# Laying out a two-layer decoder step with DMA transfers that share their engines, blocks of 3, 4, 4, 3, 3 tiles, and later norms all turned by DMA

## The chip, the cores and the metric

The kernel runs on all 8 cores of one Trainium2 chip. Each core takes one of 8 prompt sequences (2048 tokens) and 16 of 128 sample sequences (8 tokens each); the cores don't talk to each other. The metric is the device time of the slowest core in microseconds (us).

## The reference, cut to what matters

Two layers. Each has a mixer with three branches and a feed-forward part:

```python
hn = rms_norm(h, norm_mix)
proj = hn @ w_in                      # q, k, v, g_out, g_lr (rank 16), xp, u, vv, gates
g_log = log_sigmoid(g_lr @ w_gk2 + b_gk) / 16
o, s_new = gla_mix(q, k, v, g_log, s_gla, chunk)          # A: recurrence with a decaying state
branch_a = (rms_norm(o, gla_norm) * silu(g_out)) @ w_br_a
branch_b = pool_mix(xp, hist, ...) @ w_br_b               # B: trailing means 2/4/8/16, per-group map
branch_c = spatial_gate(gelu(u), gelu(vv), ...) @ w_br_c  # C: 128x128 map per chunk
h = h + (sig(ga)*branch_a + sig(gb)*branch_b + sig(gc)*branch_c) @ w_out
h = h + relu(rms_norm(h, norm_ffn) @ w_ff1)**2 @ w_ff2
```

A final RMSNorm gives y. D is 1024, the feed-forward width 4096. The states of the recurrence and of the pooling are outputs as well.

## The kernel before, in words

A core has 17 tiles of 128 tokens: tile 0 is the sample group, tiles 1 to 16 the prompt. Tiles are grouped into five blocks (`BLK`, L24), 3, 3, 3, 4 and 4 tiles; a projection that gives features on the partitions runs once per block, with 384 or 512 columns in the moving operand, so blocks set shapes and order, while the sum of the columns doesn't depend on them. All matmuls are bf16 and go through `pe_group` (its matmul is L454), all PE transposes through `pe_transposes` (L467), ACT's work through `act` (L417), VectorE's through `tt` (L425), `stt` (L428) and `vcopy` (L437).

Weights are read from HBM as f32 and cast to bf16 by transfers that GpSimd issues (POOL queue, `wload`, L675) into a ring of seven slots of 1 MB source each. The first two, the two halves of v, go in four quarters of 512 KB (`plq.dma`, L379). All other loads and stores are issued by SyncE (SP queue, L379 too).

A layer runs in stages: per block `gla_project` (rank-16 gate `wglr` and `wgk2`, v, k, q), `gla_gate` (output gate) and `gla_scan` (recurrence over the block's prompt tiles); beside them `gla_sample`, 32 steps for the sample group, each of which loads a state tile `Sf` (256 KB), casts it on GpSimd (`Sinb`), uses it on the PE and stores it; then per block `mix_block`, then twice `gate_block` over all blocks, `out_block`, and four rounds of `ff1` and `ff2`. Where the kernel starts, 17 tiles `xt` are loaded, normed to `xn`, turned on the PE and copied to `hn`, the normed activations with features on the partitions that every projection reads. The norms after `out_block` (`hx`) are turned on the PE for blocks 0 and 1 and by a DMA transpose for blocks 2 to 4; the norms after the last `ff2` of layer 1 (`fx`) are all turned by DMA. `xt` has three buffers, `xn` and `hx` two, PSUM eight banks.

The order on each engine is not the order of the source. Every operation is recorded as a node with its dependences and a cost, and `lay_out` places the nodes one by one where they could start first by those costs; each engine then gets its instructions in that order and runs them in order, waiting on semaphores. A transfer's cost there is its bytes over a rate, plus a latency; `dma_at` keeps one time per queue at which it is free, and where the other queue is busy too, half of that overlap is added. So a change of a cost, or of the blocks, moves instructions everywhere.

## Time and profile before

| | us |
|---|---|
| runs, not profiled | 2384.38, 2383.14 and one of 2616.1; median 2384.38 |
| the profiled execution, its own time | 2381.28 |
| its span (slowest core, core 5) | 2380.2 |
| spans of the other cores | 2371.6 to 2379.2 |
| PE busy in the span | 2323.0 (98%) |
| DVE, ACT, POOL busy | 1273.8, 886.3, 245.9 |

The profiled execution took 1.1 us more than the span of its slowest core, and 3.1 us less than the median of the runs. PE is TensorE; "busy" counts a matmul from its start to its modelled end, so neighbours overlap and a sum of durations is more than the time they take together. "Idle before" is what an engine stood still before an instruction, and the name behind it is what released it. PEclk, or clock, is the share of full TensorE speed that was granted: 1.00 is 2.4 GHz, and 0.50 is 1.2 GHz.

### The profile page before, as it was taken

To read this page: it belongs to the slowest core of one execution; us is meant where nothing else is said; L and a number is where in the kernel's file an instruction comes from. 1 tells how busy PE (TensorE), PEld (TensorE's weight loads), DVE (VectorE), ACT (ScalarE), POOL (GpSimd) and SP (SyncE) were. 2 spreads that over 40 slices of the span, in tenths; PEclk is the share of its full clock that TensorE was granted. 3 is DMA by queue.
4 is the path that set the end of the run, shared out by engine and by line. 5 is a ranking of instruction groups with operands and counts; after the bars stand their busy time and mean duration, and the time that the engine had idled before them with its cause. 6 is when DMAs were issued, how large, how long until landed. Compare 5 with 4: busy or idle time off the path is not lost.

```text
span 2380.2 us, 40912 instructions; the slowest of 8 cores (2371.6 to 2380.2 us)
## 1 busy us (share of the span) xinstructions
PE 2323.0 (98%) x13392; PEld 1236.5 (52%) x13392; DVE 1273.8 (54%) x2231; ACT 886.3 (37%) x1810; POOL 245.9 (10%) x266
## 2 busy tenths in 40 slices
PE   6899999999999999999999999999999999999998
PEld 4576555546445454545455555564554454545453
DVE  3787776444465444434567776744434644434355
ACT  3877753222233121212456678322222421211133
POOL 2123222000000000000012233200000000000000
PEclk9999999999999999999999999999999999999999
DMA  9554936154186040406492467451815642222112
GB/s 162 143 165 122 186 125 142 71 97 111 70 159 103 1 72 1 76 1 116 127 164 74 149 137 157 100 135 63 142 72 107 126 65 36 36 37 36 18 59 93
DMA packets 219415, 229.41 MB, mean 96 GB/s; under 512 B 54315, under 2 KB 203307, under 8 KB 216106
## 3 DMA queue, kind: packets, MB, share of 16 engines
q0 software_dynamic: 83584, 78.45, 23.8%
q1 hardware_dynamic: 135626, 148.35, 20.9%
q8 instruction: 113, 1.85, 0.3%
q14 instruction: 92, 0.75, 0.1%
HBM read 240.41 MB, written 55.05 MB: 124 GB/s over the span
## 4 chain that ended last, share of the span: by engine, by line
PE 91%; DVE 3%; issue 2%; ACT 2%; DMA 2%; POOL 0%; DVEq 0%; ACTq 0%; SPq 0%; POOLq 0%
PE ps L454 90%; DMA wring<-w_in 1%; PE ps L467 1%; DVE U L428 0%; DMA Sf<-sgla 0%; DVE Sf L428 0%; ACT rsg L417 0%; DVE tmp L428 0%; ACT L417 0%; ACT tmp L417 0%; DVE sqg L425 0%; DVE lv L815 0%; ACT Sb L417 0%; DVE pt L425 0%; ACT xj L417 0%
## 5 line engine op out<-in xcount | busy, mean ns | idle before, releaser
L454 PE MATMUL ps<-hn,wring 128*128 128x384 bf16 (+1 forms) x6400 | 1245.4, 347 | 7.8 <-DVE sgt L425 1.7
L454 PEld LDWEIGHTS ps<-hn,wring 128*128 128x128 bf16 x6400 | 621.6, 98 | 545.4 <-issue 13.4
L454 PE MATMUL ps<-wring,a 128*128 128x512 bf16 x2176 | 476.0, 379 | 0.2 <-DVE a L425 0.2
L417 ACT ACTIVATE rl<-ps 128x384 f32<-128x384 f32 (+1 forms) x320 | 169.9, 532 | 637.9 <-PE ps L454 522.2
L425 DVE TENSOR_TENSOR h<-h,ps 128x512 f32<-128x512 f32 x340 | 233.1, 687 | 277.1 <-PE ps L454 276.1
L454 PEld LDWEIGHTS ps<-wring,a 128*128 128x128 bf16 x2176 | 212.8, 98 | 255.1 <-issue 0.7
L425 DVE TENSOR_TENSOR a<-rl 128x384 bf16<-128x384 f32 (+1 forms) x320 | 194.9, 612 | 276.0 <-ACT rl L417 268.0
L417 ACT ACTIVATE sg<-ps 128x384 f32<-128x384 f32 (+1 forms) x240 | 127.9, 533 | 450.3 <-PE ps L454 322.3
L454 PE MATMUL ps<-wring,hn 128*128 128x256 bf16 (+1 forms) x1088 | 193.7, 330 | 12.2 <-DMA wring<-w_in 10.8
L425 DVE TENSOR_TENSOR tmp<-sg,ps 128x384 f32<-128x384 f32 (+1 forms) x160 | 97.3, 608 | 154.4 <-ACT sg L417 79.1
L454 PEld LDWEIGHTS ps<-wring,hn 128*128 128x128 bf16 x1088 | 105.2, 99 | 79.3 <-issue 15.3
L454 PE MATMUL ps<-OBs,wring 128*128 128x384 bf16 (+1 forms) x640 | 143.8, 347 | 0.0
L675 POOL DMA_DIRECT2D wring<-w_ff x32 | 28.0, 875 | 1047.2 <-PE ps L454 1047.2
L425 DVE TENSOR_TENSOR acc<-sg,ps 128x384 f32<-128x384 f32 (+1 forms) x80 | 48.5, 607 | 162.7 <-PE ps L454 162.7
L454 PE MATMUL ps<-H4s,wring 128*128 128x384 bf16 (+1 forms) x640 | 130.7, 347 | 0.0
L454 PE MATMUL ps<-wring,mg 128*128 128x512 bf16 x544 | 119.7, 379 | 0.0
L425 POOL TENSOR_TENSOR go<-tmp,go 128x512 bf16<-128x512 f32 x64 | 77.8, 1221 | 244.4 <-DVE tmp L428 213.0
L417 ACT ACT_TABLE_LOAD x71 | 91.1, 1283 | 26.4 <-PE ps L454 24.2
L454 PEld LDWEIGHTS ps<-H4s,wring 128*128 128x128 bf16 x640 | 62.5, 98 | 55.7 <-issue 0.3
L454 PEld LDWEIGHTS ps<-OBs,wring 128*128 128x128 bf16 x640 | 62.6, 98 | 55.0
L454 PEld LDWEIGHTS ps<-wring,mg 128*128 128x128 bf16 x544 | 52.8, 98 | 61.3
L428 DVE SCALAR_TENSOR_TENSOR tmp<-ps,vec_t,rsg 128x256 f32<-128x256 f32 x136 | 61.7, 477 | 28.6 <-ACT rsg L417 27.5
(137 smaller groups left out, 1777.6 us busy)
## 6 DMA issues: line engine op xcount, KB each, us to landing
wring<-w_ff POOLq DMA_DIRECT2D x32, 1024.0 KB, 13.1
wring<-w_in POOLq DMA_DIRECT2D x28, 1024.0 KB, 16.1
Sf<-sgla SPq DMA_DIRECT2D x64, 256.0 KB, 3.7
gla_s<-Sf SPq DMA_DIRECT2D x64, 256.0 KB, 2.8
H4s<-H_d SPq DMA_DIRECT2D x12, 768.0 KB, 8.5
OBs<-OB_d SPq DMA_DIRECT2D x12, 768.0 KB, 5.0
h_d<-h SPq DMA_DIRECT2D x17, 512.0 KB, 2.7
h<-h_d SPq DMA_DIRECT2D x17, 512.0 KB, 9.9
```

The costliest lines, as they stand in the source:

```text
L417: op(ACT, lambda: nc.scalar.activation(out=now(out), in_=now(in_), func=func, **kw), reads, writes, occ, 125.0, SETS.get(func))
L425: op(E, lambda: E.e.tensor_tensor(out=now(out), in0=now(in0), in1=now(in1), op=alu), reads, writes, occ, 90.0)
L428: op(DVE, lambda: nc.vector.scalar_tensor_tensor(out=now(out), in0=now(in0), scalar=scalar, in1=now(in1), op0=op0, op1=op1), reads, writes ...
L454: inst = nc.tensor.matmul(now(m[0]), m[1], m[2], start=m[3], stop=m[4], **kw)
L467: inst = nc.tensor.transpose(now(o), i, ident_ap)
L675: nc.gpsimd.dma_start(out=view, in_=src).then_inc(slot_sem[k], 16)
```

## The change

Six edits.

1. Blocks are 3, 4, 4, 3 and 3 tiles; the places in SBUF of the merged activations `mg` follow (`mkb`).
2. `lay_out` no longer keeps a free time per queue. A transfer enters its queue (`coming`), the queues that have something to move share the rate (`moving`), and a transfer lands (`landing`) and frees its successors when its bytes are through, plus a latency. The rates, and the cost of a DMA transpose (once its bytes instead of three times, and 1250 ns on the issuing queue), are new.
3. The rank-16 weights are padded to 32 columns on the host, so that one row of a partition is contiguous and the memset goes; they and `wgk2` are issued behind all four quarters of v.
4. `bsp` and `rep`, loads of 256 and 16 KB at the start, wait for tile 5's norm instead of a ring slot; the ring loads up to the second output-gate weight are recorded, and the gate on later `xt` loads begins, one tile later.
5. In `gate_block` the four small products that fold the pooling map into `w_br_b` (`fuse`) are recorded between the first gates instead of ahead of them.
6. All norms after `out_block` are turned by DMA.

```diff
-BLK = [(0, 3), (3, 3), (6, 3), (9, 4), (13, 4)]
+BLK = [(0, 3), (3, 4), (7, 4), (11, 3), (14, 3)]
-    w_glr = din("w_glr", [DEPTH, 128, KT, 16])
+    w_glr = din("w_glr", [DEPTH, 128, KT, 32])
...
-        dma_at = [4000.0] * 5
+        clock = 4000.0
+        coming = []
+        moving = {3: collections.deque(), 4: collections.deque()}
+        landing = []
...
+            upto = best[1] if best is not None else 1e12
+            while clock < upto and (coming or moving[3] or moving[4]):
+                on = [q for q in (moving[3], moving[4]) if q]
+                to = min([upto] + [clock + q[0][1] * len(on) for q in on] + ([max(clock, coming[0][0])] if coming else []))
+                for q in on:
+                    q[0][1] -= (to - clock) / len(on)
+                    if q[0][1] < 1e-6:
+                        m = q.popleft()[0]
+                        landing.append((to + m.lat, m.idx))
+                        landing.sort()
+                clock = to
...
             if n.byts:
-                at0 = max(dma_at[e], s + occ)
-                other = dma_at[7 - e]
-                work = n.byts / (290.0 if e == 3 else 150.0 if dma_at[4] < 20000.0 else 245.0)
-                both = max(0.0, other - at0)
-                dma_at[e] = at0 + (both + work - both / 2 if work > both / 2 else work * 2)
-                fin = dma_at[e] + (3500.0 if e == 3 else 2500.0)
+                coming.append((s + occ, n.idx, e, n.byts / (300.0 if e == 3 else 265.0) + 100.0))
+                coming.sort()
...
-            if turn:
-                n *= 3
-            record(self.E, fn, reads, writes, 500.0 if self.E is SP else 900.0, 0.0, byts=n, after=after)
+            record(self.E, fn, reads, writes, 1250.0 if turn else 500.0 if self.E is SP else 900.0,
+                   2000.0, byts=n, after=after)
...
-    mkb = [24, 30, 36, 42, 50]
+    mkb = [24, 30, 38, 46, 52]
...
-        memset(wglr.t[:, :, :], 0.0, [wglr])
...
-        plq.dma(wglr.t[:, :, 0:16], w_glr[l], writes=[wglr])
+        plq.dma(wglr.t[:, :, :], w_glr[l], writes=[wglr])
...
-        spq.dma(bsp.t[:, :, :], b_sp[l:l + 1].broadcast_to([128, 4, 128]), writes=[bsp], after=[slots[6]])
+        spq.dma(bsp.t[:, :, :], b_sp[l:l + 1].broadcast_to([128, 4, 128]), writes=[bsp], after=[hnB[5]])
...
-        if b == 0:
-            for g in range(4):
-                ps = psum()
-                pe_group([(ps.t[:, :], wpm.t[:, g, :], bbc[1][:, g, :], True, True)], [wpm, bbc[0]], [ps])
-                act(bbc[1][:, g, :], ps.t[:, :], AF.Copy, [ps], [bbc[0]])
+        def fuse(g):
+            ps = psum()
+            pe_group([(ps.t[:, :], wpm.t[:, g, :], bbc[1][:, g, :], True, True)], [wpm, bbc[0]], [ps])
+            act(bbc[1][:, g, :], ps.t[:, :], AF.Copy, [ps], [bbc[0]])
...
+                if b == 0 and pi == 0 and m4 > 1:
+                    fuse(2 * m4 - 4)
+                    fuse(2 * m4 - 3)
...
-            norm_to_hn(t, hB[t].t[:, :], hH[t], hj, hx[t % 2], turn=b >= 2)
+            norm_to_hn(t, hB[t].t[:, :], hH[t], hj, hx[t % 2], turn=True)
...
-        if t == 6:
+        if t == 7:
             wget(0, "g1")
-        spq.dma(xt[t % 3].t[:, :], rows(x_p, x_s, t), writes=[xt[t % 3]], after=[slots[4]] if t > 5 else ())
+        spq.dma(xt[t % 3].t[:, :], rows(x_p, x_s, t), writes=[xt[t % 3]], after=[slots[4]] if t > 6 else ())
...
-            wget(0, "v0")
+            wget(0, "v1")
             gla_consts(0)
```

In the two programs, all engines get the same instructions in number and shape but for these: the PE has 96 transposes of `hx` fewer, VectorE 12 copies to `hn` and one memset fewer, SP 12 DMA transposes more, and the two `wglr` loads have another shape. Three places show how the order moves. In these rows `wring` is the ring of weights, a count behind x is of instructions, and L479, L492, L450, L462 and L700 are in the changed program what L454, L467, L425, L437 and L675 are before.

On the PE at the program's start, before, from behind the third transpose on (128x256 are products of v, eight for each quarter and tile, and `xn` is turned for one tile in eight):

```order
L454 MATMUL ps<-wring,hn 128x256 x16
L454 MATMUL ps<-hn,wglr 32x384 x8
L454 MATMUL ps<-wring,hn 128x256 x16
L454 MATMUL ps<-glr,wgk_bf 128x384 x3
L467 MATMUL ps<-ident_bf,xn_71 128x128 x8
L454 MATMUL ps<-glr,wgk_bf 128x384
L454 MATMUL ps<-wring,hn 128x256 x24
L467 MATMUL ps<-ident_bf,xn_70 128x128 x8
L454 MATMUL ps<-wring,hn 128x256 x32
L467 MATMUL ps<-ident_bf,xn_71 128x128 x8
L454 MATMUL ps<-wring,hn 128x256 x16
L454 MATMUL ps<-hn,wglr 32x384 x8
```

And now, from that transpose itself on:

```order
L492 MATMUL ps<-ident_bf,xn_70 128x128 x8
L479 MATMUL ps<-wring,hn 128x256 x32
L492 MATMUL ps<-ident_bf,xn_71 128x128 x8
L479 MATMUL ps<-wring,hn 128x256 x16
L492 MATMUL ps<-ident_bf,xn_70 128x128 x8
L479 MATMUL ps<-wring,hn 128x256 x32
L492 MATMUL ps<-ident_bf,xn_71 128x128 x8
L479 MATMUL ps<-wring,hn 128x256 x24
L479 MATMUL ps<-hn,wglr 32x384 x8
L479 MATMUL ps<-wring,hn 128x256 x8
L492 MATMUL ps<-ident_bf,xn_70 128x128 x8
L479 MATMUL ps<-glr,wgk_bf 128x384 x2
```

Behind the third transpose, the rank-16 gate (`wglr`, `wgk`) stood after 16 products of v and stands now after 104, three more transposes among them; block 1's v is in that stretch too, and needs its four tiles.

On the PE in `out_block` of layer 1, before (`mg` are the blocks' merged activations, `hx` the norms turned on the PE):

```order
L454 MATMUL ps<-wring,mg_62 128x512 x48
L454 MATMUL ps<-wring,mg_63 128x512 x48
L467 MATMUL ps<-ident_bf,hx_148 128x128 x8
L454 MATMUL ps<-wring,mg_64 128x512 x8
L467 MATMUL ps<-ident_bf,hx_149 128x128 x8
L454 MATMUL ps<-wring,mg_64 128x512 x8
L467 MATMUL ps<-ident_bf,hx_148 128x128 x8
L454 MATMUL ps<-wring,mg_64 128x512 x8
L467 MATMUL ps<-ident_bf,hx_149 128x128 x8
```

The pattern goes on for six transposes in each layer. Now the five blocks stand alone:

```order
L479 MATMUL ps<-wring,mg_62 128x512 x48
L479 MATMUL ps<-wring,mg_63 128x512 x64
L479 MATMUL ps<-wring,mg_64 128x512 x64
L479 MATMUL ps<-wring,mg_65 128x512 x48
L479 MATMUL ps<-wring,mg_66 128x512 x48
```

Nothing is left between the output products; the feed-forward products follow directly.

On POOL in layer 2, where the ring is refilled for the gates while the sample steps end, before (`Sinb` is the cast of a sample state, `go` the gated output of the recurrence):

```order
L675 DMA wring<-w_in 128x8x512
L425 TENSOR_TENSOR go_78<-tmp_1_97,go_78 128x4x128
L425 TENSOR_TENSOR go_78<-tmp_0_96,go_78 128x4x128
L437 CAST Sinb_113<-Sf_111 128x512
L675 DMA wring<-w_in 128x8x512
L437 CAST Sinb_114<-Sf_112 128x512
L437 CAST Sinb_113<-Sf_108 128x512
L425 TENSOR_TENSOR go_78<-tmp_1_97,go_78 128x4x128
L425 TENSOR_TENSOR go_78<-tmp_0_96,go_78 128x4x128
L437 CAST Sinb_114<-Sf_109 128x512
L675 DMA wring<-w_in 128x8x512
```

And now:

```order
L700 DMA wring<-w_in 128x8x512
L450 TENSOR_TENSOR go_78<-tmp_1_97,go_78 128x4x128
L462 CAST Sinb_113<-Sf_109 128x512
L462 CAST Sinb_114<-Sf_110 128x512
L450 TENSOR_TENSOR go_78<-tmp_0_96,go_78 128x4x128
L462 CAST Sinb_113<-Sf_111 128x512
L700 DMA wring<-w_in 128x8x512
L450 TENSOR_TENSOR go_78<-tmp_1_97,go_78 128x4x128
L450 TENSOR_TENSOR go_78<-tmp_0_96,go_78 128x4x128
L462 CAST Sinb_114<-Sf_112 128x512
L462 CAST Sinb_113<-Sf_108 128x512
L700 DMA wring<-w_in 128x8x512
```

Before, four casts of states are left behind the first refill, and now six: five in these rows and one right behind the last of them. In layer 1 it is four before and five now.

## Rows read from the trace of the kernel before

**Rows 1.** The page: span, and busy time of each engine.
```profile
span 2380.2 us, 40912 instructions; the slowest of 8 cores (2371.6 to 2380.2 us)
PE 2323.0 (98%) x13392; PEld 1236.5 (52%) x13392; DVE 1273.8 (54%) x2231; ACT 886.3 (37%) x1810; POOL 245.9 (10%) x266
```

**Rows 2.** Busy by stretch: length, five engines, clock, DMA share, GB/s.
```profile
0.00:42.00 42.00, 20.05 (x130) 13.11 (x131) 12.44 (x25) 17.86 (x42) 12.16 (x21) 0.92 1.02 165
76.00:110.00 34.00, 27.14 (x211) 16.75 (x210) 27.55 (x42) 28.23 (x76) 6.13 (x4) 1.00 0.43 129
110.00:350.00 240.00, 230.19 (x1814) 147.64 (x1813) 185.83 (x406) 172.34 (x338) 74.31 (x80) 1.00 0.60 149
350.00:1225.00 875.00, 875.00 (x4556) 441.45 (x4555) 412.70 (x632) 226.99 (x466) 42.15 (x47) 1.00 0.44 86
1225.00:1480.00 255.00, 244.17 (x1753) 141.57 (x1752) 184.45 (x417) 189.92 (x380) 69.41 (x74) 1.00 0.54 125
1480.00:2358.00 878.00, 878.00 (x4592) 444.76 (x4590) 419.80 (x642) 225.46 (x456) 41.77 (x40) 1.00 0.35 77
2358.00:2381.00 23.00, 14.48 (x67) 6.21 (x65) 11.41 (x16) 7.10 (x19) 0.00 (x0) 0.89 0.23 91
```

**Rows 3.** Timeline of the PE, out_block of layer 1: start, length, line, operands.
```profile
698.86 0.61 PE L467 MATMUL ps<-ident_bf,hx 128*128 128x128 bf16 x8
699.30 1.89 PE L454 MATMUL ps<-wring,mg 128*128 128x512 bf16 x8
701.03 0.61 PE L467 MATMUL ps<-ident_bf,hx 128*128 128x128 bf16 x8
```

**Rows 4.** The tile hx: durations min/median/max, and its DMA landings.
```profile
L467 PE MATMUL ps<-ident_bf,hx x96: 219/219/219, 698.9 to 1872.6; 128*128 128x128 bf16 x96
L379 SPq DMA_TRANSPOSE hn<-hx x22: 1216/1218/2615, 712.9 to 1923.0; - x22
DMA to landing us min/median/max: 3.0/3.1/13.4
```

**Rows 5.** Timeline of the PE, first 42 us.
```profile
24.47 1.91 PE L454 MATMUL ps<-wring,hn 128*128 128x256 bf16 x16 [1.27 <-DMA wring<-w_in]
28.12 0.51 PE L454 MATMUL ps<-hn,wglr 128*32 128x384 bf16 x8 [1.75 <-DMA wglr<-w_glr]
36.43 5.16 PE L454 MATMUL ps<-wring,hn 128*128 128x256 bf16 x24 [4.85 <-DMA wring<-w_in]
```

**Rows 6.** Single DMA issues of the start: count, KB, us from issue to landing.
```profile
wring<-w_in POOLq DMA_DIRECT2D x1, 512.0 KB, 21.8
wglr<-w_glr POOLq DMA_DIRECT2D x1, 32.0 KB, 24.4
wgk_bf<-w_gk POOLq DMA_DIRECT2D x1, 128.0 KB, 24.5
wring<-w_in POOLq DMA_DIRECT2D x1, 512.0 KB, 31.5
wring<-w_in POOLq DMA_DIRECT2D x1, 512.0 KB, 34.5
xt<-xp SPq DMA_DIRECT2D x1, 512.0 KB, 11.2
```

**Rows 7.** Timeline of POOL and of SP at the start: issues, start and length.
```profile
1.55 1.89 POOL L379 DMA_DIRECT2D wring<-w_in  x2 [0.85 <-POOLq L149]
3.43 0.87 POOL L379 DMA_DIRECT2D wglr<-w_glr  x1
4.29 0.56 POOL L379 DMA_DIRECT2D wgk_bf<-w_gk  x1
4.84 1.79 POOL L379 DMA_DIRECT2D wring<-w_in  x2
...
11.99 10.86 SPq L379 DMA_DIRECT2D xt<-xp  x3
...
61.42 3.85 SPq L379 DMA_DIRECT2D xt<-xp  x3
```

**Rows 8.** Busy by stretch, the start once more, finer.
```profile
31.60:36.40 4.80, 0.00 (x0) 0.00 (x1) 3.60 (x4) 4.38 (x13) 0.00 (x0) 0.80 1.15 152
36.40:41.40 5.00, 4.97 (x24) 3.48 (x25) 0.00 (x0) 1.27 (x3) 0.00 (x0) 0.51 1.09 139
```

**Rows 9.** Timeline of the PE, 76 to 110 us, two of ten waits.
```profile
83.72 0.61 PE L467 MATMUL ps<-ident_bf,xn 128*128 128x128 bf16 x8 [1.48 <-DVE hn L437]
102.48 4.15 PE L454 MATMUL ps<-hn,wring 128*128 128x384 bf16 x24 [1.24 <-DVE hn L437]
```

**Rows 10.** Tile Sf, 1200 to 1500 us; its issues in all; the PE's wait.
```profile
DMA to landing us min/median/max: 2.2/3.3/14.8
Sf<-sgla SPq DMA_DIRECT2D x64, 256.0 KB, 3.7
1422.26 0.24 PE L454 MATMUL ps<-kqS,Sinb 128*128 128x8 bf16 x4 [1.12 <-POOL Sinb L437]
```

More of the change, by code:

```diff
@@ L1 @@
+import collections
 import numpy as np
@@ L270, in lay_out, with free_up @@
                 ready[num[id(n.E)]].append(n)
-        for _ in range(len(nodes)):
+        def free_up(n, fin):
+            for m in n.succ:
+                j = m.idx
+                t = fin + 250.0 if n.E is not PE or m.E is not PE else fin - n.lat
+                if t > rdy[j]:
+                    rdy[j] = t
+                need[j] -= 1
+                if need[j] == 0:
+                    ready[num[id(m.E)]].append(m)
+        while len(order) < len(nodes):
             while oldest < len(tiles_in_order) and id(tiles_in_order[oldest]) in opened:
@@ L306, in lay_out @@
                     best = pick
+            upto = best[1] if best is not None else 1e12
[9 more added lines that the diff above has]
+                clock = to
+                while coming and coming[0][0] <= clock:
+                    _, i, e, work = coming.pop(0)
+                    moving[e].append([nodes[i], work])
+                if landing and landing[0][0] < upto:
+                    upto = landing[0][0]
+            if landing and landing[0][0] <= upto:
+                at, i = landing.pop(0)
+                free_up(nodes[i], at)
+                continue
             assert best is not None, "no node can be placed"
@@ L336, in lay_out @@
             order.append(n)
-            for m in n.succ:
-                j = m.idx
-                t = fin + 250.0 if e != 0 or m.E is not PE else fin - n.lat
-                if t > rdy[j]:
-                    rdy[j] = t
-                need[j] -= 1
-                if need[j] == 0:
-                    ready[num[id(m.E)]].append(m)
+            if not n.byts:
+                free_up(n, fin)
         return max(free), order, kof
@@ L677, in fn @@
             release((slot_sem[k], 16 * slot_cnt[k]), rs, ws)
-        record(POOL, fn, (), [b] + (first[2 * k:2 * k + 2] if n in (NSLOT, NSLOT + 1) else []), 900.0 * len(todo), 0.0, byts=byts)
+        record(POOL, fn, (), [b] + (first[2 * k:2 * k + 2] if n in (NSLOT, NSLOT + 1) else []), 900.0 * len(todo), 2000.0, byts=byts)
         views[order[n][0]] = [b] + vs
@@ L1274 @@
     gk2 = gk2.reshape(DEPTH, 128, 512)
[L1275 removed]
+    glr = np.zeros((DEPTH, 128, KT, 32), np.float32)
+    glr[:, :, :, 0:16] = f(w_in)[:, :, C_GLR:C_GLR + 16].reshape(DEPTH, KT, 128, 16).transpose(0, 2, 1, 3)
     w8 = np.swapaxes(f(w_spatial)[:, :, 0:8, 0:8], 2, 3).transpose(0, 2, 1, 3).reshape(DEPTH, 8, 32)
```

3 lines of the change are left out of this document (1 added, 2 removed).

## The prediction

> **What bounds the kernel now.** I read the page first. The PE is busy 2323.0 of 2380.2 us [rows 1], so no more than 57.2 us of standing still can be won, and beside that only work of the PE that goes away, or work that runs at half clock. Then I read the busy times by stretch [rows 2], to see where the 57.2 us lie. From 350 to 1225 us and from 1480 to 2358 us the PE never stands, at clock 1.00. The idle time is 21.9 us in the first 42, 6.9 in 76 to 110, 9.8 in 110 to 350, 10.8 in 1225 to 1480 and 7.7 in the last stretch, which holds the end of the chain behind the last product. That is all of it but 0.1. The program so has two long stretches in which only the amount of PE work counts, and three short ones (start, recurrence of layer 1, recurrence of layer 2) in which the order and the arrival of data count.
>
> **The change, part by part.** The sum is made against the profiled execution, 2381.3 us, which lies 3.1 us under the median of the runs, 2384.4.
>
> *The 96 PE transposes of hx go.* They stand between output products in a stretch where the PE never waits. A group of eight transposes and one of eight products start 2.17 us apart from the next such pair (698.86 to 701.03), and the products take 1.73 of it (from 699.30 to 701.03), so eight transposes take 0.44 us [rows 3]. There are 12 groups: 12 x 0.44 = 5.3 us, all on the path. The bound below is nothing, if a wait takes their place. The 12 copies to hn that go with them were on VectorE, which has slack there: nothing.
>
> *Twelve DMA transposes come.* SP spends 1.2 us to issue one, and one lands after 3.1 us in the median and 13.4 at worst [rows 4]. The work that hides them is the rest of `out_block`: block 0 is needed again by the first `ff1`, and the first turn stood behind the products of six of 17 tiles, so that some ten tiles at 16 products of 0.216 us, 3.46 us each, are still to be done behind the first norms, over 34 us. `hx` has two buffers, so the third norm waits on VectorE for the first transpose, with the additions of later tiles behind it. In the new order of VectorE four additions lie between the first norm and the third, which the PE delivers every 1.73 us: 6.9 us, against 1.2 + 3.1 for issue and landing. If a transpose takes the worst 13.4, VectorE is late by 8 us, and eight PSUM banks at 1.73 us, 13.8 us, cover that. I take nothing, and 5 us as the upper end, should two such landings meet. A page of the Trainium skill prices the removed work differently: TensorE: Matmul & The Clock Gate (part 4, PE-mode transpose) gives about 275 ns for a 128x128 transpose inside a kernel, which would make 96 of them an estimated 26.4 us, and the change 21 us better than by the rows. The spacing of 0.44 us for eight, 55 ns each, speaks against it; 219 ns is the length of one [rows 4], and they overlap.
>
> *The start.* The POOL queue works in order, so landing times tell how long each transfer held it. The second quarter of v landed at 2.5 + 21.8 = 24.3 us, `wglr` at 3.4 + 24.4 = 27.8, `wgk2` at 4.3 + 24.5 = 28.8, the third quarter at 4.8 + 31.5 = 36.3, the fourth at 5.7 + 34.5 = 40.2 [rows 6, 7]. The small loads held the queue for 4.5 us, 3.5 of them for the 32 KB of `wglr`. With both behind v, the third quarter lands at 36.3 - 4.5 = 31.8. Before, the PE waited 1.27 us for the second quarter, 1.75 for `wglr` and 4.85 for the third [rows 5], and then its clock was at half: 24 products took 5.0 us at clock 0.51 [rows 5, 8] against 24 x 0.109 = 2.6 at full clock (16 in 1.91 us less the 0.17 of the last one's tail [rows 5]).
> Now count the work done from 24.5 us to 41.6. Before: 56 products of v, a transpose group, the rank-16 gate and four of its products, 6.1 + 0.4 + 0.4 + 0.6 = 7.5 us at full clock. In the new order, up to and with the gate, it is 104 products, three transpose groups and the gate, 11.3 + 1.3 + 0.4 = 13.0 us. They fit into 24.5 to 41.6 with 4 us of waits: the copies of tiles 3 and 4 to hn (an estimated 1 us each, by the waits for such copies [rows 9]), and tile 5, whose load was issued at 22.5 and landed 11.2 us later, at 33.7, so that it can't be turned before about 37 [rows 6, 7]. So the PE is 13.0 - 7.5 = 5.5 us ahead. One thing takes some of it back: tile 6's load, so far issued at 61.42 [rows 7], now goes out at about 28 us and shares the engines with the weights; with SP loads in flight a quarter took 36.3 - 28.8 = 7.5 us, without them 40.2 - 36.3 = 3.9. The fourth quarter then lands at about 39 and the ring's next slots as late as before, while the PE comes for them 5 us sooner. I take 5.0 us. The ends are 1 (the next slots late by 4 us) and 8 (no wait behind 24.5 us).
>
> *The first block of four tiles.* From 76 to 110 us the norms of tiles 6 to 16 come in a row, their loads only from 61.42 us on [rows 7], and the PE stands 6.9 us in ten waits, most of them on VectorE for xn and hn [rows 2, 9]. Seven tiles instead of six now lie ahead of the late ones, and products of 512 columns stand between the turns. But ACT and VectorE are busy 28.2 and 27.6 of the 34 us there, with the same work as before. So I take 2.5 of the 6.9 us. The ends are -2 and 6.
>
> *The rest of the recurrence stages*, 9.8 and 10.8 us idle, gets a new order of the same work. Nothing says which way it goes: 0, with ends of -10 and 10. The two long stretches have the same columns as before, 0. The `fuse` products move within a stretch without idle time, 0 (1 us either way). The end: the last block has three tiles, but the last tile's chain is unchanged, 0 (0.5 either way).
>
> The sum: 5.3 + 5.0 + 2.5 = 12.8. 2381.3 - 12.8 = 2368.5 in a profiled execution, and 2384.4 - 12.8 = 2371.6 as the median.
>
> **The rivals.** *Only the transposes count.* What the PE gains at the start it gives back before 350 us, since ACT and VectorE, 69 to 83% busy from 76 us on [rows 2], hold the chain of norms, gates and states. For it: their work doesn't shrink there. Against: a share of 83% with waits of 1 to 1.5 us is not a bound, and the idle time there is too small to hold 7.5 us more unless it grows. 2384.4 - 5.3 = 2379.1.
>
> *The new order is better all over.* The half of the 20.6 us in the recurrence stages goes too: 2371.6 - 10.3 = 2361.3. For it: the placing now lets two queues share, as landing times of 3.9 and 7.5 us for the same 512 KB show that they do. Against: of that idle time only 1.1 us in layer 2 is put down to a state's arrival [rows 10]; the rest waits for ACT and VectorE.
>
> *Slower: sample states arrive late during the refill.* A PE group that reads a cast state stands in order; if the state's load is late, all behind it waits. While the ring is refilled for the gates, transfers of the state tiles took up to 14.8 us against 3.3 in the median [rows 10], 11.5 us more. Before, this cost the PE 1.12 us once [rows 10], since the next steps were placed far enough behind. The new order on POOL leaves two casts more behind the first refill in layer 2, and one more in layer 1. If two of them meet such a transfer uncovered, that is 23 us: 2371.6 + 23 = 2394.6. It decides the sign from 12.8 us of such waits on. Against: five buffers of states, and loads issued a buffer ahead.
>
> *The lengths add up.* If a transpose on the PE really cost its 219 ns [rows 4], 96 of them would be 21.0 us instead of 5.3: 2371.6 - 15.7 = 2355.9. The spacing in rows 3 leaves it little. This is the direction of the page named above.
>
> **Chances and range.** The forecast, within about 5 us of 2371.6, gets 0.55; only the transposes 0.17; better all over 0.16; slower by late states 0.09; the lengths 0.03. The range takes in the first three and the milder half of the fourth: 2359 to 2385, which leaves out about 0.14. A measurement of this kernel tells 2%, 47.7 us, from no change. No case reaches 2336.7 or 2432.1; together I give these 0.03, 0.01 below and 0.02 above, where late states would have to meet in both layers.
>
> **What would show it.** In the changed kernel's profile there are no turns of hx on the PE, and `out_block` takes 58.8 us (272 x 0.216) without a gap; a wait of VectorE for hx of more than a few us would show the twelve DMA transposes uncovered. The third quarter of v lands at about 32 us and the PE's clock stays at 1.00 behind it; the idle time of the first 42 us is about 19. The idle time from 76 to 110 us is about 4. The idle time of 110 to 350 and of the recurrence of layer 2 stays near 10 each. The forecast is wrong if that grows by 5 us or more, or if the PE waits for the ring's weights between 42 and 76 us, where it never waited.

## The result, and the profile after

The change is slower, by 0.6%. That is less than the 2% that the prediction asked of a clear difference, but the interval excludes 1. Median 2394.41 us against 2384.38; the ratio is 1.0056 with a 95% interval of 1.003 to 1.0081. The ratio leaves out the runs in which half of the cores ran at a lower clock and over 1% longer, such as one of 2813.79 us here. The forecast was 2371.6, and its range ended at 2385. The profiled execution took 2399.02 us; its slowest core is now core 7 with 2398.0 us, where before it was core 5 with 2380.2. The others lie between 2369.6 and 2391.6 (before between 2371.6 and 2379.2), so the cores have come apart, though all run the same program. That is a first hint that the time now depends on how transfers happen to meet.

The page, with the rows that answer to [rows 1], the shares of the chain that ended last, and one of its groups:

```profile
span 2398.0 us, 40718 instructions; the slowest of 8 cores (2369.6 to 2398.0 us)
PE 2330.5 (97%) x13296; PEld 1234.8 (51%) x13296; DVE 1266.5 (53%) x2218; ACT 866.1 (36%) x1794; POOL 243.7 (10%) x266
...
PE 85%; DMA 6%; DVE 3%; issue 2%; ACT 2%; another core or an unknown queue 1%; POOL 0%; SPq 0%; DVEq 0%; ACTq 0%; POOLq 0%
...
L453 DVE SCALAR_TENSOR_TENSOR hx<-h,ssq,wn 128x1024 bf16<-128x1024 f32 x34 | 43.4, 1282 | 60.4 <-DMA hn<-hx 60.4
```

The PE runs 96 instructions fewer and is busy 7.5 us longer: its mean granted clock is 0.993 on core 7 and was 0.998 on core 5, so more of its work ran at half clock. VectorE stood 60.4 us at the two `hx` buffers until a turn by DMA had landed. Busy by stretch on core 7, columns as in [rows 2]:

```profile
0.00:42.00 42.00, 29.80 (x232) 21.88 (x233) 15.38 (x27) 19.81 (x45) 11.84 (x21) 1.00 1.01 177
42.00:76.00 34.00, 30.28 (x228) 20.52 (x226) 19.86 (x54) 22.40 (x47) 0.00 (x0) 1.00 1.10 173
76.00:110.00 34.00, 32.73 (x224) 17.95 (x223) 29.62 (x42) 30.66 (x73) 2.33 (x2) 1.00 0.47 132
110.00:350.00 240.00, 225.92 (x1765) 144.49 (x1764) 188.16 (x404) 157.51 (x321) 79.57 (x84) 0.99 0.62 150
350.00:700.00 350.00, 350.00 (x1902) 184.95 (x1901) 158.43 (x262) 92.08 (x181) 21.19 (x22) 1.00 0.49 108
700.00:760.00 60.00, 52.62 (x246) 24.50 (x244) 31.83 (x40) 18.95 (x48) 1.75 (x2) 0.95 0.97 129
760.00:1225.00 465.00, 464.99 (x2336) 227.62 (x2335) 209.92 (x316) 113.14 (x235) 15.11 (x20) 1.00 0.35 63
1225.00:1480.00 255.00, 241.76 (x1707) 138.64 (x1705) 177.51 (x404) 176.22 (x366) 67.75 (x75) 0.98 0.56 132
1480.00:1850.00 370.00, 370.00 (x2028) 195.72 (x2027) 181.72 (x303) 97.97 (x180) 32.78 (x29) 1.00 0.42 100
1850.00:1960.00 110.00, 102.86 (x485) 47.17 (x483) 59.17 (x79) 36.51 (x88) 3.49 (x4) 0.98 0.82 134
```

The start is what it was to be and more: 12.2 us idle in the first 42 instead of 21.9, and 1.3 instead of 6.9 from 76 to 110. What is new are two holes in the stretches that had none, 7.4 us in 700 to 760 and 7.1 in 1850 to 1960. Both lie around `out_block` and the first `ff1`. The tile `hx` on core 7 in layer 1 against [rows 4], the PE's waits there, and what engines waited for from 700 to 760 us:

```profile
L405 SPq DMA_TRANSPOSE hn<-hx x17: 1216/1227/7730, 692.1 to 762.1; - x17
  DVE hx L453: 31.2, 6
DMA to landing us min/median/max: 3.0/3.3/19.7
...
715.95 20.84 PE L479 MATMUL ps<-wring,mg 128*128 128x512 bf16 x88 [3.63 <-DVE h L450]
756.12 8.76 PE L479 MATMUL ps<-hn,wring 128*128 128x512 bf16 x32 [3.75 <-ACT rl L442]
...
DVE hx L453 <- DMA hn<-hx: 30.6, 5, 11.3
ACT hj L442 <- DVE h L450: 27.3, 6, 16.5
...
ACT rl L442 <- DVE a L450: 11.5, 2, 10.3
```

Read it as a chain: a turn lands late, VectorE stands at `hx`, and the additions `h` and squares `a` queued behind it on VectorE are not done. At the first hole the PE then runs out of PSUM banks, at the second ScalarE runs out of `rl` buffers. On core 1 the chain of waits shows it whole, in order of time (start, length, what; short pieces left out):

```profile
689.41 1.29 DVE hx L453
...
690.77 13.41 DMA hn<-hx
...
704.27 1.30 DVE hx L453
...
705.63 5.46 DMA hn<-hx
...
711.53 0.69 DVE h L450
...
712.35 15.71 PE ps L479 x72
```

Behind the first hole on core 7 the PE's clock falls to half for a while: in the 6 us after the wait that ended at 715.95 the mean granted clock is 0.72, then it is full again. That does not follow every hole. On core 1 a wait of 3.50 us ended at 750.70, and from 745 to 763 us the clock stays at 1.00.

```profile
716.00:722.00 6.00, 6.00 (x21) 2.39 (x22) 6.00 (x9) 4.23 (x11) 0.00 (x0) 0.72 0.58 115
722.00:728.00 6.00, 6.00 (x30) 2.70 (x29) 5.69 (x7) 4.23 (x11) 0.00 (x0) 1.00 0.54 105
```

To compare kernels I cut every core's execution in each layer at the first product of the gates, at the first and the last of `out_block`, and in layer 1 at the last of `ff2`. The stages in us, slowest core of each profile and means of the eight:

| stage | before, core 5 | after, core 7 | before, mean | after, mean |
|---|---|---|---|---|
| to the first gate product | 384.0 | 377.9 | 379.7 | 374.7 |
| gate, layer 1 | 294.1 | 294.5 | 294.1 | 294.6 |
| out_block, layer 1 | 61.2 | 64.0 | 61.2 | 60.2 |
| ff, layer 1 | 472.4 | 478.2 | 472.4 | 477.0 |
| recurrence and mixing, layer 2 | 334.8 | 341.5 | 334.9 | 340.5 |
| gate, layer 2 | 294.1 | 294.7 | 294.1 | 294.8 |
| out_block, layer 2 | 61.2 | 60.4 | 61.2 | 59.0 |
| from there to the end | 478.4 | 486.8 | 478.4 | 483.2 |

The slowest core's 17.8 us are -6.1 at the start, +16.2 in the four rows of out_block and ff, +6.7 in layer 2's recurrence, +1.0 in the gates. The mean of the cores is 8.0 us longer: -5.0, +6.2, +5.6 and +1.2.

Layer 2's recurrence, stretch 1225 to 1480, is longer by two things that the rows show. The PE stands 13.2 us in it on core 7, where it stood 10.8 on core 5, and its clock is 0.98 there, where it was 1.00 on every core before. Half clock follows waits for sample states there:

```profile
PE ps L479 <- POOL Sinb L462: 8.5, 3, 6.1
...
1431.72 0.24 PE L479 MATMUL ps<-kqS,Sinb 128*128 128x8 bf16 x4 [3.23 <-POOL Sinb L462]
...
1433.00:1439.00 6.00, 5.20 (x21) 2.33 (x20) 3.44 (x10) 0.00 (x0) 2.32 (x4) 0.50 0.98 284
```

The first of these rows is the PE's wait for states in layer 1 (100 to 400 us), 8.5 us of which 6.1 in one wait; in layer 2 it is 4.2.

### The profile page after: what moved, and what is told of

Read it like the earlier page. It is cut to its first block, busy times and chain, and to the rows that moved or that the text cites. A ratio compares the mean times of both kernels' runs of the same rounds, so it can differ in the third digit from the quotient of the medians.

```text
span 2398.0 us, 40718 instructions; the slowest of 8 cores (2369.6 to 2398.0 us)
## 1 busy us (share of the span) xinstructions
PE 2330.5 (97%) x13296; PEld 1234.8 (51%) x13296; DVE 1266.5 (53%) x2218; ACT 866.1 (36%) x1794; POOL 243.7 (10%) x266
## 4 chain that ended last, share of the span: by engine, by line
PE 85%; DMA 6%; DVE 3%; issue 2%; ACT 2%; another core or an unknown queue 1%; POOL 0%; SPq 0%; DVEq 0%; ACTq 0%; POOLq 0%
PE ps L479 84%; DMA hn<-hx 3%; DMA gla_s<-Sf 1%; DMA Sf<-sgla 1%; PE ps L492 1%; DMA wring<-w_in 1%; DVE hx L453 1%; ACT L442 0%; ACT rsg L442 0%; DMA xt<-xp 0%; DMA pool_s<-xptok 0%; DVE Sf L453 0%; DVE tmp L453 0%; DVE h L450 0%
## 5 line engine op out<-in xcount | busy, mean ns | idle before, releaser
L479 PE MATMUL ps<-hn,wring 128*128 128x384 bf16 (+1 forms) x6400 | 1254.4, 349 | 13.3 <-ACT rl L442 4.7
L479 PEld LDWEIGHTS ps<-hn,wring 128*128 128x128 bf16 x6400 | 625.1, 98 | 557.2 <-issue 28.3
L479 PE MATMUL ps<-wring,a 128*128 128x512 bf16 x2176 | 476.7, 379 | 1.7 <-DVE a L450 1.7
L450 DVE TENSOR_TENSOR h<-h,ps 128x512 f32<-128x512 f32 x340 | 231.6, 687 | 261.6 <-PE ps L479 261.6
L479 PEld LDWEIGHTS ps<-wring,a 128*128 128x128 bf16 x2176 | 212.5, 98 | 257.0 <-issue 3.5
L450 DVE TENSOR_TENSOR a<-rl 128x384 bf16<-128x384 f32 (+1 forms) x320 | 194.4, 611 | 257.4 <-ACT rl L442 252.0
L479 PE MATMUL ps<-wring,hn 128*128 128x256 bf16 (+1 forms) x1088 | 193.1, 329 | 4.5 <-DVE hn L462 2.0
L450 DVE TENSOR_TENSOR tmp<-sg,ps 128x384 f32<-128x384 f32 (+1 forms) x160 | 97.0, 608 | 161.3 <-PE ps L479 95.3
L479 PEld LDWEIGHTS ps<-wring,hn 128*128 128x128 bf16 x1088 | 105.4, 99 | 72.1 <-issue 7.5
L479 PE MATMUL ps<-OBs,wring 128*128 128x384 bf16 (+1 forms) x640 | 141.5, 347 | 0.0
L700 POOL DMA_DIRECT2D wring<-w_ff x32 | 28.0, 875 | 1063.8 <-PE ps L479 1055.1
L450 DVE TENSOR_TENSOR acc<-sg,ps 128x384 f32<-128x384 f32 (+1 forms) x80 | 48.6, 607 | 157.0 <-PE ps L479 157.0
L479 PE MATMUL ps<-H4s,wring 128*128 128x384 bf16 (+1 forms) x640 | 130.7, 347 | 0.0
L479 PE MATMUL ps<-wring,mg 128*128 128x512 bf16 x544 | 119.7, 383 | 5.3 <-DVE h L450 5.3
L450 POOL TENSOR_TENSOR go<-tmp,go 128x512 bf16<-128x512 f32 x64 | 76.4, 1201 | 240.9 <-DVE tmp L453 178.7
L479 PEld LDWEIGHTS ps<-OBs,wring 128*128 128x128 bf16 x640 | 62.6, 98 | 55.3
L479 PEld LDWEIGHTS ps<-H4s,wring 128*128 128x128 bf16 x640 | 62.5, 98 | 54.7
L479 PEld LDWEIGHTS ps<-wring,mg 128*128 128x128 bf16 x544 | 53.5, 99 | 71.0 <-issue 8.5
L453 DVE SCALAR_TENSOR_TENSOR hx<-h,ssq,wn 128x1024 bf16<-128x1024 f32 x34 | 43.4, 1282 | 60.4 <-DMA hn<-hx 60.4
```

The costliest lines, as they stand in the source:

```text
L450: op(E, lambda: E.e.tensor_tensor(out=now(out), in0=now(in0), in1=now(in1), op=alu), reads, writes, occ, 90.0)
L453: op(DVE, lambda: nc.vector.scalar_tensor_tensor(out=now(out), in0=now(in0), scalar=scalar, in1=now(in1), op0=op0, op1=op1), reads, writes ...
L479: inst = nc.tensor.matmul(now(m[0]), m[1], m[2], start=m[3], stop=m[4], **kw)
L700: nc.gpsimd.dma_start(out=view, in_=src).then_inc(slot_sem[k], 16)
```

## The experiments

All ratios are to the kernel before, run beside each. "The change" stands at 1.0056. "Hx wait" is VectorE's for a turn at that tile over a whole execution, "state wait" the PE's for POOL's `Sinb`; both are ranges over cores. The ff stage is layer 1's unless said otherwise, a single figure is the mean of the cores, and "the end" is the table's last row. Before: hx wait 1.2 to 5.5, state wait 0.2 to 2.2. The change: hx wait 35.7 to 60.4, state wait 9.8 to 14.8.

### One edit out, or one edit alone

**Turns of blocks 0 and 1 back on the PE**, the rest of the change kept.
```diff
-            norm_to_hn(t, hB[t].t[:, :], hH[t], hj, hx[t % 2], turn=True)
+            norm_to_hn(t, hB[t].t[:, :], hH[t], hj, hx[t % 2], turn=b >= 2)
```


> The change with edit 6 undone: the norms of blocks 0 and 1 behind out_block are turned on the PE again, and all is laid out anew. Theory A (the DMA turns land late and stop VectorE, then the PE): 5.3 us of PE work come back, the 14.5 us that the PE stood in the two out_block stretches on core 7 and some 5 us of half clock behind them go, so about 2394 + 5 - 20 = 2380, and VectorE waits under 5 us for hx. Theory B (the turns are hidden, the new order of the recurrence alone is what costs): 2394 + 5 = 2399.

1.0077 (1.0062 to 1.0093), nearer to theory B's number but not by its cause. The hx wait is down to 1.2 to 8.3, and the ff stage still takes 475.3 to 479.9 us and the end 480.9 to 485.3. So it is not the twelve added turns alone that cost: of the ten in each layer that stay with the DMA, the last ones land late too (7.2, 13.2 and 10.6 us on core 7), and ScalarE now stands for them. Its buffers `rl` lie where the second `hx` buffer lies, and it waits 17.8 to 23.1 us there for turns to land, against 2.0 to 5.2 in the change.

**The turns alone**, in the kernel before, the same line the other way round.

> The kernel before with edit 6 alone: all norms behind out_block turned by DMA, old placing, old blocks. Theory A: 2384 - 5 + 20 = 2399 if the first turns land as late as in the change (13 to 20 us), less if the old, dearer cost of a turn in the placing keeps them apart. Theory B: 2384 - 5 = 2379, as the prediction had it.

1.0025 (1.0013 to 1.0036). Each `out_block` gains 2.7 us (61.2 to 58.5), as forecast, but ff takes 474.6 to 481.7 and the end 481.4 to 487.6. More is lost than gained: theory A's sign, at less than half of its size.

**The change without the new placing**: `lay_out` and the reckoning of transfers as before. The part of the edit on transfers:
```diff
-            record(self.E, fn, reads, writes, 1250.0 if turn else 500.0 if self.E is SP else 900.0,
-                   2000.0, byts=n, after=after)
+            if turn:
+                n *= 3
+            record(self.E, fn, reads, writes, 500.0 if self.E is SP else 900.0, 0.0, byts=n, after=after)
```


> The change with edit 2 undone: the old lay_out with its rates and its 3500 ns behind an SP transfer, and a DMA turn at three times its bytes; all else as changed. Theory A: the start keeps its gain (idle time of the first 42 us about 12), the state casts wait less (POOL for Sf about 60 us instead of 108), the PE's wait for them falls from 12.7 to under 4 us; the turns still cost, so about 2394 - 9 = 2385. Theory B: 2379 or less, since the placing is what costs.

1.0091 (1.0071 to 1.011); neither theory. out_block and ff are clean in layer 1 (58.5, 472.4), but the first stage takes 391.6 on the mean and layer 2's recurrence 343.4, with state waits of 12.8 to 22.6, where theory A had them fall under 4.

**The change with the old blocks** (3, 3, 3, 4, 4).
```diff
-BLK = [(0, 3), (3, 4), (7, 4), (11, 3), (14, 3)]
+BLK = [(0, 3), (3, 3), (6, 3), (9, 4), (13, 4)]
```


> The change with edit 1 undone: blocks of 3, 3, 3, 4, 4 tiles. If the blocks matter, as the prediction had it with 2.5 us, the idle time from 76 to 110 us rises from 1.3 towards 6.9 us, and the time to about 2397. Rival (four tiles in block 1 crowd VectorE and the states of the recurrence): 2388 or less.

1.0091 (1.0075 to 1.0107): 388.7 to the first gate instead of 374.7, so the blocks are worth 14 us there within the change. The state wait is gone with them, 3.0 at most.

**The new placing alone** in the kernel before.

> The kernel before with nothing but the new reckoning of transfers (edit 2): old blocks, 16-column rank weights, 112 norms turned on TensorE as before. Theory P (the new placing brings the late sample states and part of the ff stage's loss, whatever the blocks and the turns): each recurrence stage about 5 us longer, PE's wait for POOL's Sinb 10 us or more instead of 1.1, ff stage of layer 1 at 475 or more instead of 472; ratio about 1.005 (2396). Rival Q (the loss needs the change's mix of turns and blocks; the placing alone is worth its start): 2375 to 2385, Sinb wait under 5 us.

1.0143 (1.0128 to 1.0158), 392.4 to the first gate. Theory P is right on ff (480.4) and wrong on its means: the state wait is 2.1 at most. The end takes 484.6. So the placing alone, without one turn more on the DMA, costs 14 us in ff and the end. VectorE's hx wait is 10.0 at most here; on core 7 it is ScalarE that stands for a late turn, VectorE's squares behind it, and then the PE:

```profile
ACT rl L442 <- DMA hn<-hx: 11.8, 1, 11.8
...
DVE a L450 <- ACT rl L442: 8.9, 2, 8.7
...
PE ps L479 <- DVE a L450: 5.9, 1, 5.9
```

**The new blocks alone** in the kernel before.

> The kernel before with blocks of 3, 4, 4, 3, 3 tiles and their places in memory, nothing else. Theory A (blocks interact with the placing: under the old reckoning they lose at the start, as the change without the new placing did, 391 us to the first gate instead of 380): 2395 or more. Rival B (blocks help by themselves, as they did within the change, where leaving them out cost 14 us): 2370 to 2380.

1.03 (1.0257 to 1.0343), 434 us to the first gate. Theory A by sign, and nothing like it in size. State waits 15.3 to 21.2. ff is clean (472.4). Taken together: late states go with the new blocks (6 to 23 us on the cores of every kernel with them, 2 to 11 where the states are reckoned later; with old blocks at most 3.5 in five kernels, 7.6 and 9.7 in two), the start needs blocks and placing together, and each of them alone costs 13 or 54 us there.

### Where the ff stage's loss is

**A third `hx` buffer.**
```diff
-            norm_to_hn(t, hB[t].t[:, :], hH[t], hj, hx[t % 2], turn=True)
+            norm_to_hn(t, hB[t].t[:, :], hH[t], hj, hx[t % 3], turn=True)
```


> The change with three buffers for the normalised tile instead of two (places 59, 24, 28 KB); in the order only one piece at each out_block's end moves on PE. Theory A (behind out_block DVE stands at its two-buffer wait for a turn that lands late, and PE then at DVE's additions): DVE's 60 us of waits for turns at hx fall below 30, the PE wait of 3.6 us before the first ff block goes, the two ff stages get 2 to 6 us shorter each, ratio about 0.996 to 0.998 of the change. Rival B (the third place lies under the relu's buffers, so ScalarE waits there instead): hx waits fall, ACT's rl wait grows above 5 us, ff stages as in the change.

1.008 (1.0068 to 1.0092). The hx wait fell to 18.0 to 42.0, the PE's `rl` wait on core 7 rose from 4.7 to 14.1, and ff is no shorter, 479.4 against 477.0. Rival B: the wait moved.

**`rl` moved away from `hx`**, and the junk tile `fj` to 26 KB.
```diff
-    rl = [sba(f"rl{i}", [128, 512], F32, at(24 + 2 * i)) for i in range(4)]
+    rl = [sba(f"rl{i}", [128, 512], F32, at(28 + 2 * i)) for i in range(4)]
```


> The change with the relu's four buffers moved from 24..32 KB to 28..36 KB and the ff junk tile to 26 KB, so that the relu no longer waits for the last turns to read the second hx buffer. Theory A (the DVE wait for a turn is the loss, the relu's only its echo): PE's wait for ACT rl (4.7 us) goes, but that for DVE h stays about 4 to 8 us; ff stages shorter by 0 to 3 us. Rival B (the overlap of the buffers is the loss): the ff stages fall back to 472 and the last stage to 478, 2388.

1.0117 (1.0099 to 1.0134), ff 481.7. Rival B falls. Core 2, 735 to 765 us:
```profile
ACT rl L442 <- DVE a L450: 11.2, 2, 9.9
DVE hx L453 <- DMA hn<-hx: 10.6, 1, 10.6
PE ps L479 <- DVE a L450: 6.7, 3, 4.4
```
With no shared place left, ScalarE waits for VectorE's squares, and these for VectorE's norm. More or other buffers don't help here, since the landing stays late.

**Turns reckoned at three times their bytes** in the change.
```diff
-                   2000.0, byts=n, after=after)
+                   2000.0, byts=n * 3 if turn else n, after=after)
```


> The change with each turn reckoned at three times its bytes (as before's table did), nothing else. Theory A (the ff stage's loss comes because the new reckoning holds a turn for short and puts the last norms closely behind out_block, where the two 1 MB refills of the ring slow each turn's landing to 10-17 us): with dearer turns the last norms come later, after the refills have landed; ff stages of both layers fall back towards 472 and 478, 6 us or more in all; ratio about 0.996 to 0.998 of the change's (2385 to 2390). Rival B (DVE's order with four and more norms in a row behind each other makes longer waits for the two buffers): hx waits grow and the ff stages stay at 475 or more. The recurrence is to stay as in the change, by either.

1.0054 (1.0026 to 1.0082). ff is 479.1, as rival B had it, but the hx wait halves (19.5 to 33.1) where B had it grow. VectorE now has the last five norms in one row. The size of the hx wait alone doesn't tell what the PE loses.

**Two ring refills held back.** In all kernels here, each turn of `hx` that took more than 7 us to land had a 1 MB refill of the ring in flight beside it. Two of these refills (for `a11` and `b10`) are issued when `out_block` frees their places, at 722 to 737 us by core in the change, and first read over 110 us later. Here they wait for the last turn, and the planner is told so (`after=behind` on the same node).
```diff
+        behind = [hnB[NTILE - 1]] if order[n][0][1] in ("a11", "b10") else []
         def fn(rs, ws, lt):
             acquire(POOL, rs, ws)
+            for h in behind:
+                POOL.wait(h.w)
```


> The change with the ring refills a11 and b10 (the two 1 MB loads that start when out_block's last tile frees their places) held back until the last turn has landed; both are first read over 60 us later. Theory A (the ff stages lose because turns and refills share the DMA engines: landing 10 to 20 us instead of 3): the turns behind out_block land in 3 to 5 us, DVE's wait at hx falls from 36-60 us to under 20 in layer 1, the ff stages fall towards 472 and 479, total 2386 to 2390. Rival B (the earlier refills, those of the last gate weights around 673 us, and the h loads are what they meet): the first turns stay late, ff stages as in the change, 2394.

Theory A for ff. 1.0017 (1.0007 to 1.0027), 2387.47: 0.4% is back. The PE's order is the change's but for one place in each layer, and ff takes 472.4 us on all eight cores, the end 479.1. VectorE's order of the last norms and squares moved too, and no run holds the refills in the old order. Core 7 again, the POOL queue, the tile `hx`, and the PE by stretch:
```profile
752.81 1.75 POOL L704 DMA_DIRECT2D wring<-w_ff  x2 [77.92 <-DMA hn<-hx]
...
  DVE hx L453: 15.9, 5
DMA to landing us min/median/max: 3.0/3.1/18.3
...
700.00:760.00 60.00, 57.26 (x274) 27.02 (x273) 39.19 (x50) 21.68 (x53) 1.75 (x2) 0.97 0.73 121
760.00:1225.00 465.00, 465.00 (x2347) 228.81 (x2346) 206.83 (x314) 112.38 (x233) 15.99 (x22) 1.00 0.38 68
```
The second hole is gone. The first, 2.7 us here, is not, and the landing of 18.3 belongs to it: the first turns meet the gate's last refills, issued at 665, 673 and 674 us. So the first turns stay late, as rival B had it for them. `out_block` still takes 58.3 to 64.3 us by core.

**The turns alone, with the two refills held**, in the kernel before.

> The kernel before with all 34 first norms turned by DMA and the two refills held back as in the kernel above. Theory A (without the collision the turns are worth the 2.7 us that each out_block gains): ff stages 472 and 478 to 479, out_blocks 58.5, recurrences as before: ratio 0.997 to 0.998 (2378 to 2380). Rival B (the collision with the gate's last refills is the one that costs): 1.0025 as with the turns alone.

0.9989 (0.9979 to 0.9998), 2381.46. Theory A by stage: out_blocks 58.5, ff 472.4, the end 479.5, layer 2's recurrence 334.6. From 640 to 1100 us the PE stands nowhere:
```profile
640.00:1100.00 460.00, 460.00 (x2290) 223.84 (x2288) 206.26 (x305) 102.10 (x209) 16.62 (x19) 1.00 0.40 65
```
From 725 to 800 us the turns of core 1 land as follows, first in the kernel before, then with the turns alone, then here:
```profile
DMA to landing us min/median/max: 3.1/3.1/14.3
...
DMA to landing us min/median/max: 3.0/3.1/16.6
...
DMA to landing us min/median/max: 3.1/3.1/3.3
```
Against the turns alone, PE, ScalarE, SP and POOL have the same order, and VectorE has some squares ahead of the last norms. The landings are what that order doesn't explain. The first of the three rows says something else as well: the slowest landing beside these refills took 13 to 15 us on every core of the kernel before, and the PE lost nothing by it. What a late landing costs depends on how much stands in order behind it.

The total misses the expected 0.997 to 0.998, because the first stage takes 382.3 us instead of 379.7 and the end 1.1 more. It is the fastest kernel here, by 0.1%, and it has one edit of the change and one that the change lacks.

**The first block's turns back on the PE**, refills held.

> The change with the refills held back, and the first block's three tiles of each out_block turned on TensorE again (48 transposes, 2.6 us in all). Theory A (the first turns, issued around 692 us beside the last gate refills and the h loads, hold DVE and so out_block on some cores): out_block of layer 1 at 59.8 to 60.5 on all cores instead of 58.3 to 64.3, DVE's wait at hx under 8 us, total 2 to 4 us below the change with held refills (2384). Rival B (the wait only moves to the fourth tile's turn): out_block still 60 to 65 on some cores, 2387 to 2390.

1.002 (0.999 to 1.005). `out_block` is even now, 59.6 to 60.7 on all cores, and the hx wait 8.6 to 17.9, so the first turns were what spread it. The total is not lower: layer 2's recurrence takes 343.8 on the mean, against 340.5 with the refills held alone, in an order of the PE that is the same there. That is a measure of how far this stage scatters between executions of one order.

### The start and the recurrence

**Sample states reckoned 1500 ns later.**
```diff
-                spq.dma(s.t[:, :, :], sgla[l, i, 2 * hp:2 * hp + 2].rearrange("h d e -> d h e"), writes=[s])
+                spq.dma(s.t[:, :, :], sgla[l, i, 2 * hp:2 * hp + 2].rearrange("h d e -> d h e"), writes=[s], lat=3500.0)
```


> The change with 3500 ns instead of 2000 ns reckoned behind the landing of each of the 64 sample-state loads, nothing else. Theory A (the states come late because the new reckoning puts their use too close behind their load): PE's wait for POOL's Sinb falls from 10-15 us to under 5, each recurrence stage about 4 us shorter than the change's, total about 2387. Rival B (they come late because five buffers cycle and ring refills share the DMA engines with them, however the use is placed): waits stay at 8 us or more, total within 2 us of the change.

1.005 (1.0037 to 1.0063). The state wait falls to 2.9 to 10.8, and on four cores layer 2's recurrence to 336 to 338 us; on the other four it stays at 340 to 343.5. Theory A for the wait; the stage follows it on half of the cores, and the total not at all.

**The same with the refills held.**

> The change with the two refills held back and 3500 ns reckoned behind each sample-state load. Theory A: what the two edits gave apart adds up, 2380 to 2386. Rival B (the recurrence is a draw of the placing, in which another latency is only another draw): second recurrence at 338 to 343 again, the total no better than with the refills alone.

1.0016 (1.0004 to 1.0028), recurrence 338.1 to 342.1: rival B by its outcome. The state wait is down to 2.4 to 8.8, and the recurrence is as long as with refills held alone (340.4 on the mean against 340.5). That does not clear the states: on core 7 another late transfer took their place. A store of `go` to HBM was in flight for 19.49 us, ScalarE waited for it at `xfS`, and the PE for ScalarE.
```profile
1417.28 19.49 DMA H_d<-go
...
PE ps L479 <- ACT xfS L442: 4.2, 1, 4.2
```

**Another draw of the order**, in the change and in the kernel before: a random rank of up to 4 places on each step, with the reckoned cost of an activation-table swap left at 400.
```diff
-        _, order, kof = min((lay_out(seed) for seed in range(ORDERS)), key=lambda r: r[0])
+        _, order, kof = min((lay_out(seed) for seed in (1,)), key=lambda r: r[0])
```


> The change with its order laid once more with a random rank of up to 4 places added to every step (seed 1, the swap cost kept), nothing else. Theory C (the placing is a draw: orders that differ in near ties scatter by as much as the change's whole effect): differs from the change by 6 us or more, either way. Rival D (the loss is systematic): within 3 us of the change, 2391 to 2397.

> The kernel before with the same random rank of up to 4 places (seed 1). Theory C (a draw): slower than before by 5 us or more, since before stands at the good end of its draws. Rival D: within 3 us of before.

1.0313 (1.0267 to 1.0358) and 1.0259 (1.0212 to 1.0306). Theory C: 432 us to the first gate in both, and layer 2's recurrence went from 334.9 to 342.3 in the kernel before by this draw alone. ff keeps what each kernel has, 477.9 and 472.4. Core 7 of the kernel before, SP and busy from 60 to 80 us, and then the same core with the new draw, SP, the PE, and busy by stretch:
```profile
60.72 35.66 SPq L379 DMA_DIRECT2D xt<-xp  x9
...
60.00:80.00 20.00, 19.00 (x154) 12.73 (x151) 16.08 (x44) 17.86 (x43) 0.00 (x0) 1.00 0.96 173
...
65.11 35.77 SPq L379 DMA_DIRECT2D xt<-xp  x11
...
80.51 1.01 PE L467 MATMUL ps<-ident_bf,xn 128*128 128x128 bf16 x8 [25.64 <-DVE xn L428]
...
60.00:80.00 20.00, 0.00 (x0) 0.00 (x0) 2.65 (x6) 3.89 (x8) 0.00 (x0) 0.50 0.91 164
80.00:100.00 20.00, 7.08 (x56) 5.41 (x56) 13.18 (x15) 10.83 (x30) 0.00 (x0) 0.50 0.57 181
```
The loads behind the ring's gate go out 4.4 us later, but the PE turns the first tile behind them at 80.51 us and in the kernel before at 79.02. What differs is what the PE has in the meantime: before, it does projections and the recurrence of block 0 from 55 us on; in the new draw eleven turns of `xn` stand in order ahead of that work. So the PE is empty from 55 to 80 us, and its clock is at half behind it.

**The start's edits** on before's placing and blocks, with turns and held refills.

> The kernel before with its own placing and blocks, but with the start's edits, the fuse's place, all turns by DMA and the two refills held. Theory A (the start's edits gain by themselves what was forecast, 5 us): to the first gate 375 against 380, total 2375. Rival B (start's edits and order hang together: with the old placing and new blocks they cost 12 us, and the order around them decides): 385 or more to the first gate, total 2386 or more.

1.0015 (1.0005 to 1.0025), 387.2 us to the first gate against 382.3 with turns and refills only. Rival B: these edits gain nothing by themselves here, they cost 5 us (one order of each, so a draw may be part of it). The moved `fuse` shows too: 294.5 us or more per gate stage in every kernel that has it, 294.1 without it where nothing disturbs.

## Why the prediction was wrong, point by point

- **The PE transposes: right.** 5.3 us forecast; 2.7 us in each out_block, 5.4, with the turns alone and wherever nothing stood.
- **"Twelve DMA transposes come ... I take nothing, and 5 us as the upper end": this step failed.** Against out_blocks of 58.5, ff of 472.4 and an end of 478.4, the change's slowest core lost 21.6 us, the mean 11.6. The argument priced one landing at the worst 13.4 us seen and covered it with eight PSUM banks. The change moved the first turn from 712.9 to 692.1 us on the slowest core, next to refills issued at 665 to 674 us. The first two turns there landed in 15.4 and 19.7 us, VectorE stood through both (10.0 and 4.5 us), and the PE lost 3.6. On core 1 the banks ran out at 711. The bank count so was about right and the landing's price was not. The larger loss is one that the argument didn't look at: behind out_block, turns met a second pair of refills. Such landings were there before (13.4 and 10.5 us on core 5, for turns 6.1 us apart) and cost nothing; now two of 14.1 and 12.6 us came 2.4 us apart, and the norms behind them had to wait with the squares of `ff1`. The runs with held refills show it: ff is back at 472.4 on all cores, with no landing over 6.3 us behind out_block. The Trainium skill, "DMA: Bandwidth & Descriptors", in its rules for kernel authors, says that issuing engines don't bring engines of their own: all share the same 16 and interleave. This case's trace agrees: POOL issued the refills, SP the turns, and these landed in 3.0 us at best and in 19.7 beside the refills.
- **The start (5.0) and 76 to 110 us (2.5): sum right, reading wrong.** To the first gate the change gains 5.0 us on the mean and 6.1 on the slowest core. The idle time of the first 42 us is 12.2, where about 19 was forecast. Then 3.7 us of waits appear between 42 and 76 us, most of it one for the ring's weights (1.11) and one for ScalarE's `lv` (2.14), 76 to 110 gives 5.6 instead of 2.5, and 110 to 350 loses 4.3. The edits I credited lose 5 us without the new blocks and placing. The terms can't be added one by one: of the three parts (placing, blocks, start's edits) every partial set measured is 13 to 59 us slower to the first gate than all together.
- **Layer 2's recurrence: 0 with ends of 10; it was +5.6 on the mean.** Within its ends, by waits and by a clock of 0.98 to 0.99 behind them that the term didn't hold. The kernel before has a good draw there, 334.9; its second draw has 342.3, and every kernel with new blocks or new placing 339 to 345.
- **The rival that came nearest** named the sample states, 2394.6. That its number was the result's is luck, since it added one mechanism to gains of 12.8 us that did not come in full, and left out the ff stage. But its mechanism did happen: the PE's wait for states went from 1.1 us on core 5 to 12.7 on core 7, 8.5 of it in layer 1 and 4.2 in layer 2, in waits of up to 6.1 and not 11.5, and with half clock behind some of them. The waits come with the new blocks. Taking most of them away left the recurrence as long, because other waits came.
- **The long stretches "have the same columns as before, 0": this failed as well.** The new placing alone, with no turn added, costs 14 us there, because it moves the turns that stay with the DMA too. On core 7 the clock added to it: 0.72 in the 6 us behind the first hole.

What stays open: why layer 2's recurrence is some 5 us longer in every kernel with new blocks, new placing or a new draw, while the three others with before's placing and blocks have 334.6 to 335.2. The rows above show waits for late transfers and half clock behind them, but no run takes these away together. Nor is it known why the stage varies between the cores of one program, by 2 us in the change and by up to 12 in its second draw. No kernel here has the first turns clear of the gate's refills together with the change's start.

## What to carry to other kernels

When work is moved from an engine to the DMA queues, look up which transfers are under way at the new time, and price the landing beside them; then ask which engine stands in order behind that landing. A transfer that is needed late should not be issued just because its place is free: holding two refills back for some 20 us was worth 0.4%, more than the 5.4 us of the transposes that went. And where a planner lays the order, an edit's worth is that of one draw: lay the unchanged kernel a second time before believing a difference of a few us.

## What the runs showed of the hardware

- A transpose by DMA of a 256 KB tile lands in 3.0 us at best and in up to 19.7 beside 1 MB loads of another queue; on core 7 of the change the 256 KB state loads took 3.7 in the median and 13.7 at worst in layer 2.
- One wait of 3.63 us, in a PE that was busy for 350 us ahead of it, was followed by 6 us at a mean granted clock of 0.72, which is half clock for part of them; one of 3.50 us on core 1 by none below 1.00; and a wait of 25.64 us, in the new draw of the kernel before, by 20 us at 0.50. With less to do, the PE of the change's slowest core was busy 7.5 us longer.
